# A two-layer hybrid block: the start of the program in another order, its first norm vector spread by TensorE and its first two weight panels split by halves

## The reference

```
xn   = RMSNorm(x) * pre_mix_g
proj = xn @ w_in          -> u_lru | g_lru | q | k | v | two merge gates
A    = (RG-LRU(conv4(u_lru)) * gelu(g_lru)) @ w_pa
B    = sliding-window attention(rope(q), rope(k), v, sinks) @ w_pb
x   += RMSNorm((sigmoid(gA)*A + sigmoid(gB)*B) @ w_o)
x   += RMSNorm(SwiGLU(RMSNorm(x)))
```

## Time and profile before

| | |
|---|---|
| Time, median of 3 | 854.84 us (854.8 to 855.02) |
| Span of the profiled execution, first to last instruction | 852.7 us |
| TensorE busy | 816.7 us, 96% |
| VectorE, ScalarE, GpSimd busy | 536.4, 418.3, 60.6 us |
| Mean granted TensorE clock | 0.996 |

### The profile page before, as it was taken

How to read it: one execution, slowest core, us unless ns; L and a number is a source line. 1 busy time by engine, 2 the same in 40 slices (tenths; PEclk the granted TensorE clock), 3 DMA queues, 4 the chain that set the end, 5 groups by cost and what they waited for, 6 DMA issues and landing times.

```text
span 852.7 us, 10305 instructions
## 1 busy us (share of the span) xinstructions
PE 816.7 (96%) x4217; PEld 690.4 (81%) x4217; DVE 536.4 (63%) x544; ACT 418.3 (49%) x540; POOL 60.6 (7%) x125
## 2 busy tenths in 40 slices
PE   3799999999989999999989999999999899999996
PEld 3698899888867888888869988988887788888885
DVE  5597799546585455545477959875565655554642
ACT  4345887643354344443353678765235334443431
POOL 6411000000010000000021400000001000000000
PEclk9999999999999999999999999999999999999999
DMA  8575444444445565564428845444453474655511
GB/s 290 158 241 208 151 166 169 152 148 153 144 151 201 199 238 197 191 202 152 148 68 257 292 148 192 155 148 149 148 187 108 149 271 168 222 166 195 186 50 49
DMA packets 79998, 148.59 MB, mean 174 GB/s; under 512 B 7120, under 2 KB 27728, under 8 KB 79952
## 3 DMA queue, kind: packets, MB, share of 16 engines
q1 hardware_dynamic: 79536, 147.93, 51.7%
q10 hardware_dynamic: 416, 0.02, 0.0%
HBM read 146.88 MB, written 1.05 MB: 173 GB/s over the span
## 4 chain that ended last, share of the span: by engine, by line
PE 87%; DVE 4%; POOL 3%; ACT 2%; issue 2%; DMA 1%; POOLq 0%; SPq 0%; DVEq 0%; ACTq 0%
PE work L574 16%; PE work L576 16%; PE work L575 16%; PE acc L574 7%; PE acc L575 7%; PE acc L576 7%; PE work L566 4%; PE work L568 4%; PE work L567 4%; PE acc L638 2%; ACT weights_hi L849 1%; PE work L661 1%; PE work L707 1%; DVE q_tok L1183 1%; POOL mean_square_eps L447 1%
## 5 line engine op out<-in xcount | busy, mean ns | idle before, releaser
L1176 DVE TENSOR_TENSOR weights_lo<-weights_raw,weights_hi 128x2048 fp32r<-128x2048 f32 x134 | 306.5, 2292 | 171.9 <-ACT weights_hi L849 171.4
L849 ACT ACTIVATE weights_hi<-weights_raw 128x2048 fp32r<-128x2048 f32 x134 | 256.3, 1915 | 230.8 <-PE work L576 130.1
L574 PE MATMUL work<-weights_hi,act_a_hi 128*128 128x512 f32 x544 | 215.1, 395 | 5.2 <-DVE weights_lo L1176 3.5
L576 PE MATMUL work<-weights_hi,act_a_lo 128*128 128x512 f32 x544 | 212.2, 390 | 0.0
L575 PE MATMUL work<-weights_lo,act_a_hi 128*128 128x512 f32 x544 | 212.0, 390 | 0.0
L574 PEld LDWEIGHTS work<-weights_hi,act_a_hi 128*128 128x128 f32 x544 | 102.2, 188 | 28.1 <-DVE weights_lo L1176 4.8
L576 PEld LDWEIGHTS work<-weights_hi,act_a_lo 128*128 128x128 f32 x544 | 102.1, 188 | 21.6
L575 PEld LDWEIGHTS work<-weights_lo,act_a_hi 128*128 128x128 f32 x544 | 102.2, 188 | 20.4
L574 PE MATMUL acc<-weights_hi,act_b_hi 128*128 128x512 f32 x240 | 94.3, 393 | 0.0
L576 PE MATMUL acc<-weights_hi,act_b_lo 128*128 128x512 f32 x240 | 93.5, 390 | 0.0
L575 PE MATMUL acc<-weights_lo,act_b_hi 128*128 128x512 f32 x240 | 93.5, 389 | 0.0
(11 more groups left out here) (161 smaller groups left out, 883.1 us busy)
## 6 DMA issues: line engine op xcount, KB each, us to landing
weights_raw<-in_w_in SPq DMA_DIRECT2D x44, 1024.0 KB, 5.6
weights_raw<-in_w_ffn_down SPq DMA_DIRECT2D x22, 1024.0 KB, 4.7
weights_raw<-in_w_ffn_gate SPq DMA_DIRECT2D x20, 1024.0 KB, 5.1
weights_raw<-in_w_ffn_up SPq DMA_DIRECT2D x20, 1024.0 KB, 5.1
weights_raw<-in_w_pa SPq DMA_DIRECT2D x8, 1024.0 KB, 4.9
weights_raw<-in_w_pb SPq DMA_DIRECT2D x8, 1024.0 KB, 4.9
weights_raw<-in_w_o SPq DMA_DIRECT2D x8, 1024.0 KB, 4.7
weights_raw<-in_w_ffn_gate SPq DMA_DIRECT2D x4, 512.0 KB, 3.8
```

The lines of the kernel that those rows point to most:

```text
L574: mm(dst, xh, wh, start=first, stop=False)
L576: return mm(dst, xl, wh, start=False, stop=final)
L849: activate(w_hi[:, SLOT[n], :], raw[:, n % RAW, :], ACT.Copy).then_inc(hi_done.sem, 1)
L1176: v.tensor_tensor(w_lo[:, SLOT[n], :], raw[:, n % RAW, :], bits(w_hi[:, SLOT[n], :]), ALU.subtract).then_inc(split_done.sem, 1)
```

## The change

- `pre_mix_g[0]` comes as one row of 4 KB into partition 0 (`temps`, on ACT's queue). PE multiplies a column of ones by it (two products of 512 columns, one row deep) into `acc[2]` and `acc[3]`, and DVE's first two norms read the gain there. The broadcast for layer 0 falls away; later ones stay.
- Panel 0 is loaded and split in two halves; panel 1 is loaded whole and split in halves. Tile 0's norm is done in halves too. PE multiplies half by half.
- SP's order: x tile 0, the two halves, x tile 1, panel 1, the rows of the vectors, panel 2.
- In layer 0 PE does `kv` for tile 0, `kv` for tile 1, the vectors' transpose (now into `acc[1]`), then `q0`, each panel for both tiles.
- Decay rates, sinks and the layer's vectors are made by DVE after `split_lo` 5; the angles, sines and first rope after `split_lo` 7; the other ropes one by one after the convolutions. POOL waits for the layer's vectors.
- The loop over layers is written out, as layer 0 has its own form.

```
--- the start, SP
             sp.dma_start(xres[:, 0, :], x[0, 0:P, :]).then_inc(x_loaded[0], 16)
-            sp.dma_start(g_pre[:, :], pre_mix_g[0].partition_broadcast(P)).then_inc(pre_loaded.sem, 16)
-            load(0, 0)
+            first_half(0, 0).then_inc(head_loaded, 16)
+            first_half(0, 1).then_inc(raw_loaded[0].sem, 16)
             sp.dma_start(xres[:, 1, :], x[0, P:S, :]).then_inc(x_loaded[1], 16)
+            load(0, 1)
...
-            for n in range(1, RAW):
-                load(0, n)
+            load(0, 2)
--- PE, start
+            pe.wait_ge(ones_done, 1)
+            pe.wait_ge(gain_row, 16)
+            for h in range(2):
+                spread = mm(acc[:, 2 + h, :], ones_row, GT[0:1, h, :], start=True, stop=True)
+            spread.then_inc(gain_spread, 1)
             pe.wait_ge(ident_done, 1)
-            turn_x(0, 0, "xn", 0)
-            pe.wait_ge(rows_loaded, 16 * 5)
-            nc.tensor.transpose(acc[:, 3, 0:P], vec_rows[:, :], ident[:, :]).then_inc(vec_turned, 1)
...
--- PE, layer 0
+                def first_products():
+                    for j in range(2):
+                        pe.wait_ge(head_split, j + 1)
+                        pe.wait_ge(*xa_done.at(l, j + 1))
+                        t_panel_product("kv", j, acc[:, 0, :], xn_hi, xn_lo, 0, range(0, 2))
+                        split_ready(AT["kv", j])
+                        ins = t_panel_product("kv", j, acc[:, 0, :], xn_hi, xn_lo, 0, range(2, 4))
+                        if j == 0:
+                            turn_x(l, 0, "xn", 1)
+                    ins.then_inc(tile0.sem, 1)
+                    pe.wait_ge(*xa_done.at(l, 4))
+                    for j in range(2):
+                        t_panel_product("kv", j, acc[:, 2, :], xn_hi, xn_lo, 1).then_inc(panel_used.sem, 1)
+                    pe.wait_ge(rows_loaded, 16 * 5)
+                    nc.tensor.transpose(acc[:, 1, 0:P], vec_rows[:, :], ident[:, :]).then_inc(vec_turned, 1)
+                    for j in range(2):
+                        split_ready(AT["q0", j])
+                        if j == 0:
+                            pe.wait_ge(vec_copied, 1)
+                        ins = t_panel_product("q0", j, acc[:, 1, :], xn_hi, xn_lo, 0)
+                        if j == 1:
+                            ins.then_inc(tile0.sem, 1)
+                        t_panel_product("q0", j, acc[:, 3, :], xn_hi, xn_lo, 1).then_inc(panel_used.sem, 1)
...
-                pe.wait_ge(*rope_read.at(l, 2))
+                pe.wait_ge(*rope_read.at(l, 3 if first else 2))
--- ACT, start
             act.wait_ge(x_loaded[0], 16)
             mean_square(0, xres[:, 0, :], ms_done.sem, 1)
+            act.wait_ge(head_loaded, 16)
+            half_hi(0, 0).then_inc(head_hi, 1)
+            act.wait_ge(*raw_loaded[0].at(0, LOADED[0]))
+            half_hi(0, 1).then_inc(hi_done.sem, 1)
             xa_hi(0, 0, "xn", 0)
-            split_hi(0, 0)
             act.wait_ge(x_loaded[1], 16)
             mean_square(1, xres[:, 1, :], ms_done.sem, 2)
+            act.wait_ge(*raw_loaded[1].at(0, LOADED[1]))
+            half_hi(1, 0).then_inc(head_hi, 1)
+            half_hi(1, 1).then_inc(hi_done.sem, 1)
+            xa_hi(0, 0, "xn", 1)
+            for n in range(2, 4):
+                split_hi(0, n)
             act.wait_ge(exp_ready, 1)
             activate(sp_t[:, :, :], sp_s[:, :, :], ACT.Exp, scale=-1.0).then_inc(exp_done, 1)
--- DVE, start
+            dve.wait_ge(gain_spread, 1)
+            dve.wait_ge(rstd_done.sem, 1)
+            for h in range(2):
+                cols = slice(512 * h, 512 * h + 512)
+                v.scalar_tensor_tensor(QTOK[:, 0, cols], xres[:, 0, cols], rstd[:, 0:1], acc[:, 2 + h, :],
+                                       ALU.mult, ALU.mult).then_inc(xs_done.sem if h else head_normed, 1)
+            dve.wait_ge(head_hi, 1)
+            half_lo(0, 0).then_inc(head_split, 1)
+            xa_lo(0, 0, "xn", 0, range(1))
+            dve.wait_ge(*hi_done.at(0, 1))
+            half_lo(0, 1).then_inc(split_done.sem, 1)
+            xa_lo(0, 0, "xn", 0, range(1, 2))
+            dve.wait_ge(rstd_done.sem, 2)
+            v.scalar_tensor_tensor(QTOK[:, 1, :], xres[:, 1, :], rstd[:, 1:2],
+                                   acc[:, 2:4, :].rearrange("p b f -> p (b f)"),
+                                   ALU.mult, ALU.mult).then_inc(xs_done.sem, 1)
+            dve.wait_ge(head_hi, 2)
+            half_lo(1, 0).then_inc(head_split, 1)
+            dve.wait_ge(*hi_done.at(0, 2))
+            half_lo(1, 1).then_inc(split_done.sem, 1)
+            xa_lo(0, 0, "xn", 1)
+            split_lo(0, 2)
...
--- DVE, layer 0 (decay_rates, sink_columns, layer_vectors, angles hold the moved lines)
+                    if first and (name, j) == ("kv", 1):
+                        decay_rates()
+                        sink_columns()
+                        layer_vectors()
+                    if first and (name, j) == ("q0", 1):
+                        angles()
+                        rope("kv", 0)
                     if name == "u":
                         conv(j)
+                    if first and name == "u" and j < 3:
+                        rope(*ROPES[1 + j])
```

More of the change, by code:

```diff
@@ L503, in _, with layer @@
             pool.wait_ge(history_done, 1)
-            def layer(l, last):
+            def layer(l, first, last):
+                pool.wait_ge(*vec_ready.at(l, 1))
                 for c in range(KD):
@@ L545, in claim, with layer @@
                 return work[k % 4]
-            pe.wait_ge(ident_done, 1)
-            turn_x(0, 0, "xn", 0)
-            pe.wait_ge(rows_loaded, 16 * 5)
-            nc.tensor.transpose(acc[:, 3, 0:P], vec_rows[:, :], ident[:, :]).then_inc(vec_turned, 1)
-            def layer(l, last_layer):
+            pe.wait_ge(ones_done, 1)
[3 more added lines that the diff above has]
+            spread.then_inc(gain_spread, 1)
+            pe.wait_ge(ident_done, 1)
+            for h in range(2):
+                dst = claim(0, "xn", h)
+                if h == 0:
+                    pe.wait_ge(head_normed, 1)
+                else:
+                    pe.wait_ge(*xs_done.at(0, 1))
+                for k in range(4):
+                    f = (4 * h + k) * P
+                    ins = nc.tensor.transpose(dst[:, k * P:k * P + P], QTOK[:, 0, f:f + P], ident[:, :])
+                ins.then_inc(turned.sem, 1)
+            def layer(l, first, last_layer):
                 def split_ready(n):
@@ L1184, in normed, with xa_lo @@
                                        ALU.mult, ALU.mult).then_inc(xs_done.sem, 1)
-            def xa_lo(l, first, name, t):
-                for h in range(2):
+            def xa_lo(l, first, name, t, halves=range(2)):
+                for h in halves:
                     m = first + 2 * t + h + 1
@@ L1230, in _ @@
[L1230 to L1242, removed]
-            for i in range(2):
-                for par in range(2):
-                    rows = slice(64 * i, 64 * i + 64)
-                    own(v.tensor_copy(sinks[rows, :, 0, 4 * par:4 * par + 4], by_head[rows, :, :, i, par]))
@@ L1247, in _, with layer @@
-            own(v.tensor_scalar(sinks[:, :, 1, :], sinks[:, :, 0, :], -1.0, None, ALU.mult))
-            dve.wait_ge(sines_done, 1)
+            split_lo(0, 3)
             dve.sem_clear(dve_step)
-            def layer(l, last_layer):
+            def layer(l, first, last_layer):
                 step[0] = 0
@@ new lines, in sink_columns @@
+                def sink_columns():
+                    dve.wait_ge(sinks_loaded, 16)
+                    by_head = sink_rows[:, :, :].rearrange("p l (g i r) -> p l g i r", i=2, r=2)
+                    for i in range(2):
+                        for par in range(2):
+                            rows = slice(64 * i, 64 * i + 64)
+                            own(v.tensor_copy(sinks[rows, :, 0, 4 * par:4 * par + 4], by_head[rows, :, :, i, par]))
+                    own(v.tensor_scalar(sinks[:, :, 1, :], sinks[:, :, 0, :], -1.0, None, ALU.mult))
@@ L1272, in conv, with layer_vectors @@
+                def layer_vectors():
+                    signalled(v.tensor_copy(vec[:, :, :], vecs[:, bass.ds(l, 1), :, :]
+                                            .rearrange("p o v k -> p (o v) k")), *vec_ready.at(l, 1))
+                    own(v.tensor_copy(sink[:, :, :], sinks[:, bass.ds(l, 1), :, :].rearrange("p o n h -> p (o n) h")))
                 def conv(j):
```

127 lines of the change are left out of this document (79 added, 48 removed).

## The result

The changed kernel took **844.3 us** (median, 843.78 to 844.83) beside 854.93 us for the kernel before on the same chip: ratio 0.9873, 95% interval 0.9859 to 0.9887. In a later comparison, on another chip, it was 844.94 beside 855.29 (0.988, 0.9864 to 0.9897). The forecast was 844.2.

A forecast was written before the change was run, and what follows sets the result against it. TensorE, busy 96% of the span, was taken as the bound, so time gained before `u` is kept. Terms 4.25 + 5.1 + 1.4 + 0.6 - 0.85 gave about 10.6 us; 852.7 - 10.6 + 2.1 = 844.2 us, range 842.7 to 847.6.

The forecast's parts named there:

- Earlier start: Head: gain as a row and panels by halves bring TensorE's first product to 11.1 instead of 15.34, 4.25 us.
- The stall: TensorE's wait before tile 1, behind VectorE's wait for the angles, goes: 5.1 us from start to start.
- its low clock: Seven product starts at 1.2 GHz after the stall, 34.89 to 37.9, go with it: 1.4 us.
- The first low clock: Three products fewer at TensorE's low clock after the first product, 0.2 us each: 0.6 us gained.
- The vectors: Added TensorE wait before `q`, for the vectors' transpose, VectorE's two copies and the way back: 0.85 us lost.
- VectorE behind q: Small work, angles and ropes moved behind `q`; convolution 0 ends at 52.9, needed 53.9: cover 1.0 us.
- GpSimd's angles: Angle reduction on GpSimd slips between VectorE instructions, done by about 36, needed at 42.4; cost 0 to 2.
- B: VectorE becomes the bound in the `u` stage, 1 to 3 us lost: 846.2; chance 0.19.
- C: Head later, gain's row at 5.0 or second half panel at 10.4, or both: 846 to 847.3; chance 0.15.
- D: Weight supply gives back half the gain, as weights are asked for 10.6 us earlier: 849.5; chance 0.05.
- E: TensorE stays at 1.2 GHz through many short waits in the head, so slower: 861.6; chance 0.02.

The follow-up runs named there:

- u_broadcast: The changed kernel with the gain's 512 KB broadcast back between x and the first half panel, without the two spreading products: 846.25 us.
- u_whole: The changed kernel with panels 0 and 1 loaded and split whole, and the old order on ScalarE and VectorE: 849.44 us.
- i_head: The changed kernel with position conversion behind norm 0, a signal per spreading product, and ScalarE's tile 0 first-half high part ahead of panel 0's second half: 843.94 us.
- b_tile1_first: The kernel before with one line moved: VectorE makes tile 1's low part ahead of its wait for the angles: 851.43 us.
- u_angles: The changed kernel with the wait for the angles and their clamp back ahead of tile 1's low part on VectorE: 856.32 us.
- i_vectors: The changed kernel with the vectors' transpose right behind tile 1's transposes and VectorE's copies ahead of panel 2's low part: 843.47 us.
- f_two: The changed kernel with two superfluous VectorE instructions of 128 x 2048 ahead of the angles in layer 0: 846.37 us.
- u_order: The changed kernel with layer 0's old product order: `kv` and `q0` for tile 0, then for tile 1: 847.97 us.
- f_one: The changed kernel with one superfluous VectorE instruction of 128 x 2048 ahead of the angles in layer 0: 844.58 us.
- i_warm: The changed kernel with early vectors' transpose, earlier head, tile 1's root ahead of angle work, and nine identity transposes before the first product: 842.3 us.

## Why the prediction was right

**The method.** One event, the start of `u`, was taken to carry the time. It does: the rest is 805.4 to 805.6 us in 12 of 14 traces, with a TensorE head that differs by 14 us, and the two exceptions are those with waits inside the `u` stage. The loop, now written out and costed at 0, is in that rest too: 805.6 against 805.5.

**Earlier start (4.25 us by the sum).** 15.34 - 11.25 = 4.1. The parts were sized well: the row of the gain was there at 3.24 (3.4 taken; 2.2 to 3.5 over the traces), the spreading products took 3.75 us (3.4), the first half's high part began at 6.40 (6.95), the second's at 8.84 (8.65). The row took 2.5 us from issue to landing, 1.5 to 2.8 over the eleven traces that have it; the fixed 2.0 us that the prediction cites from the Trainium skill stand there for DMAs issued by GpSimd, and this one is ScalarE's. u_broadcast gives the row 1.7 us at the first product, which comes at 12.95 with the second half landing at 10.5; the prediction had 12.9 for a landing at 10.4. u_whole gives the rest of the idea 4.5 us, but that is the halves, the order on ScalarE and VectorE and a late position vector together. The two prices don't add up to 4.1, as each run leaves the other part in.

**What I missed there.** Norm 0 did not wait for the gain or the root but for the position vector. VectorE's first instructions in the changed kernel:

```profile
7.21 0.17 DVE L1268 CAST pos_float<-pos_int 128x2 f32<-128x2 int32 x1 [7.21 <-DMA pos_int<-in_positions]
...
7.30 1.41 DVE L1279 SCALAR_TENSOR_TENSOR q_tok<-x_residual,rstd,acc 128x512 f32<-128x512 f32 x2
```

The conversion of the positions stands first in VectorE's stream, and the vector came at 7.2 instead of 5.0, once its transfer was issued behind the gain's row and flew beside the weights. It cost only 0.3 us against my 7.0, and nothing at the first product, since the activations' high part stands behind the second half's on ScalarE (8.84 to 9.81). i_head took both away: the first product came 1.5 us earlier, and `u` no earlier.

**The stall (5.1) and its low clock (1.4).** Right in size in the sum, and b_tile1_first and u_angles show that it isn't a quantity of its own: alone it is worth 3 to 4.6 us, and put back into the new order it costs 12.6 at the start of `u` (49.27 against 36.63) and 11.4 in the medians.

**The first low clock (0.6).** It lasted 3.1 us, 3.8 taken, and before it had lasted 5.3 (15.34 to 20.63 in the earlier trace rows), not the 4.9 that I read. So there were 7 slow products instead of 12, where I had 9, and the term was 1.0. That it came out so near, and on the good side, was luck within a spread of 2.9 to 5.5 us. With it the terms as measured are 4.1 + 5.1 + 1.3 + 1.0 - 0.8 = 10.7, of the 10.8 us by which `u` starts earlier. The step from the span to the median, taken as 2.1, was 2.3 (844.3 - 842.0).

**The vectors (0.85).** 24.62 to 25.43, 0.81 us. i_vectors shows that it could be had for the transpose alone.

**VectorE behind q.** I gave 1.0 us of cover; it was 1.9. ScalarE's timeline and VectorE's (against the earlier trace rows) show the term that was wrong:

```profile
38.56 1.28 ACT L961 ACT_TABLE_LOAD   x1
...
44.43 0.58 ACT L1113 ACTIVATE lru_u<-work 128x512 f32<-128x512 f32 x1
...
49.06 2.75 DVE L1388 SCALAR_TENSOR_TENSOR lru_uc<-lru_u,vectors_of_layer,lru_uc 128x256 f32<-128x256 f32 x6
```

There is a table load ahead of the sines, hidden, but none behind them, so the copy of `u` 0 follows the sines at once and convolution 0 ends at 51.8 instead of 52.9. A load seen between two instructions in one order of the program need not be there in another.

**GpSimd's angles.** Expected done at 36, done at 28.7 in fact:

```profile
26.02 2.29 POOL L499 TENSOR_SCALAR turned_by<-turns 128x64 f32<-128x64 f32 x1
...
28.39 0.33 POOL L500 TENSOR_TENSOR angle<-angle,turned_by 128x64 f32<-128x64 f32 x1
```

The mechanism, one small instruction per split, is there (2.29 us beside the split of 25.66), but most of the chain ran in VectorE's pauses and beside its halves. It was off the path either way.

**Rivals.** B and C did not decide; f_two gives the price of the first, and u_broadcast that of a late second half. D did not occur: no wait for a panel is among those of the changed kernel up to 110 us. E, TensorE at 1.2 GHz through the head, did not occur in full; the spread of the first low stretch is its small form.

## What to carry to other kernels

When one engine is busy from some point on, take the first event behind the start-up, write the chains of all engines up to it, and compare kernels by the time of that event; small parts add up there to 0.2 us. A wait's price is what the waiting engine could have done instead: the same wait for the angles was 4.9 us in one order and 9.6 in another, and taking it away alone gave 3 to 4.6 of its 6.5 us, because VectorE, which made it late, had more to do behind it. When an engine's stream starts with something that nobody urgent needs (here the positions on VectorE, the angles on GpSimd ahead of a root), look there first. And a run that takes a part back tells its price only if it takes nothing else back with it: ours of the halves took the order on two engines along.

## What was not expected of the hardware

The low level of TensorE's clock after the first product lasted 2.9, 3.1, 3.1, 3.1, 3.3, 3.7, 3.9, 4.4, 4.5, 4.8, 5.2, 5.3 and 5.5 us in thirteen traces, with about 0.47 us lost for each us of products at that level (0.2 of 0.43). Seven of them (the changed kernel twice, u_order, u_angles, i_vectors, f_one, f_two) have the same program up to there and show 3.1 to 5.2 us. So single traces differ by up to 1.0 us with no cause in the program, and part of what u_whole and u_order lose in their traces is this. The Trainium skill, "TensorE: Matmul & The Clock Gate", section "Part 1: The HAM clock gate", says that the number of slow products at a start varies from run to run of one kernel; the traces agree, with 3.1 and 3.9 us in two of the changed kernel. With TensorE kept at work beforehand it was 0.9 us in the one trace of i_warm.

The position vector, 1 KB, took 4.3 us from issue to landing before and 5.9 in the changed kernel, where it was issued 0.55 us later; 4.2 to 4.4 in the three traces where it is first in ScalarE's queue, 5.8 us and more, up to 6.9, behind the gain's row. u_broadcast, with the halves beside it but first in the queue again, has 4.2, which speaks for its place; but there the broadcast stands ahead of the halves, so that the traffic beside it differs as well, and the two are not separated.
